# A hybrid decoder step on one core: reordered work at the first input tiles and at the last output tiles

## What is computed

```python
h = rms_norm(x, norm_mix_pre)
rq, rk, rv, rg, aq, ak, av, gr, ga = split_columns(h @ w_in, IN_WIDTHS)
# branch A: multi-scale retention; branch B: dilated window attention in three groups
mix = sigmoid(gr) * (r @ w_branch_ret) + sigmoid(ga) * (att_o @ w_branch_attn)
x = x + rms_norm(mix @ w_out, norm_mix_post)
u = rms_norm(x, norm_ffn_pre) @ w_ffn_up
c = conv_b + sum(conv_w[i] * ext[:, i:i + T] for i in range(3))
f = (gelu(c[..., :D_FF]) * c[..., D_FF:]) @ w_ffn_down
x = x + rms_norm(f, norm_ffn_post)       # y_prompt and y_sample
```

## Time and profile before

| what | value |
|---|---|
| median of 3 runs | 1087.83 us (1085.61 to 1088.73) |
| profiled execution, its own time | 1086.23 us |
| span of that execution, first to last instruction | 1084.4 us |
| mean granted TensorE clock | 0.981 of full speed |
| PE busy | 1014.0 us, 94% of the span |
| DVE, ACT, POOL busy | 541.8, 383.5, 197.3 us |

### The profile page before, as it was taken

How to read it: one execution, slowest core, us unless ns; L and a number is a source line. 1 busy time by engine, 2 the same in 40 slices (tenths; PEclk the granted TensorE clock), 3 DMA queues, 4 the chain that set the end, 5 groups by cost and what they waited for, 6 DMA issues and landing times.

```text
span 1084.4 us, 20154 instructions
## 1 busy us (share of the span) xinstructions
PE 1014.0 (94%) x7666; PEld 882.5 (81%) x7666; DVE 541.8 (50%) x865; ACT 383.5 (35%) x842; POOL 197.3 (18%) x382
## 2 busy tenths in 40 slices
PE   5999999999997799999998888999999999999994
PEld 3777777768875699998887668999999999777773
DVE  5353233423237777765116266676667666422214
ACT  5333231441431433323223364444444443212312
POOL 2102003414133234334310100000000000011003
PEclk9999999999998899999999989999999999999998
DMA  6744425426496566564651612545554544221322
GB/s 225 263 158 161 165 102 202 175 89 232 183 297 205 167 202 200 183 203 146 228 174 59 219 59 95 208 165 174 167 202 171 174 154 145 81 84 64 112 90 85
DMA packets 40768, 175.34 MB, mean 162 GB/s; under 512 B 7242, under 2 KB 7690, under 8 KB 39168
## 3 DMA queue, kind: packets, MB, share of 16 engines
q1 hardware_dynamic: 25472, 125.78, 33.4%
q0 software_dynamic: 15232, 48.65, 14.0%
HBM read 164.40 MB, written 54.05 MB: 201 GB/s over the span
## 4 chain that ended last, share of the span: by engine, by line
PE 78%; DMA 6%; ACT 6%; DVE 5%; issue 2%; POOL 2%; SPq 0%; DVEq 0%; ACTq 0%; POOLq 0%
PE bank L1280 10%; PE bank L1282 9%; PE bank L1281 9%; PE bank L1759 8%; PE bank L1760 8%; PE bank L1761 8%; PE bank L1353 4%; PE bank L1355 4%; PE bank L1354 4%; DMA qbc<-sample_queries 3%; PE bank L1299 3%; DMA wraw<-in_weights 2%; ACT whi L782 1%; DMA kvv<-in_cache_kv_g 1%; DVE wlo L1836 1%
## 5 line engine op out<-in xcount | busy, mean ns | idle before, releaser
L1836 DVE TENSOR_TENSOR wlo<-wraw,whi 128x1024 fp32r<-128x1024 f32 x89 | 108.9, 1225 | 353.2 <-ACT whi L782 353.1
L782 ACT ACTIVATE whi<-wraw 128x1024 fp32r<-128x1024 f32 x91 | 96.4, 1059 | 391.8 <-PE bank L1282 247.6
L1759 PE MATMUL bank<-T1h,whi 128*128 128x288 f32 (+1 forms) x704 | 202.4, 288 | 3.1 <-DVE T1l L1846 1.7
L1760 PE MATMUL bank<-T1l,whi 128*128 128x288 f32 (+1 forms) x704 | 203.6, 289 | 0.0
L1761 PE MATMUL bank<-T1h,wlo 128*128 128x288 f32 (+1 forms) x704 | 203.2, 289 | 0.0
L1280 PE MATMUL bank<-whi,T1h 128*128 128x512 f32 (+1 forms) x352 | 142.3, 404 | 7.7 <-DVE etmp L1981 7.6
L1281 PE MATMUL bank<-wlo,T1h 128*128 128x512 f32 (+1 forms) x352 | 137.1, 390 | 0.0
L1282 PE MATMUL bank<-whi,T1l 128*128 128x512 f32 (+1 forms) x352 | 136.7, 388 | 0.0
L1759 PEld LDWEIGHTS bank<-T1h,whi 128*128 128x128 f32 x704 | 133.0, 189 | 3.8 <-issue 1.9
L1760 PEld LDWEIGHTS bank<-T1l,whi 128*128 128x128 f32 x704 | 132.7, 189 | 0.0
L1761 PEld LDWEIGHTS bank<-T1h,wlo 128*128 128x128 f32 x704 | 132.3, 188 | 0.0
(11 more groups left out here) (302 smaller groups left out, 1828.0 us busy)
## 6 DMA issues: line engine op xcount, KB each, us to landing
wraw<-in_weights SPq DMA_DIRECT2D x142, 512.0 KB, 3.6
out_s_kv_g<-in_cache_kv_g SPq DMA_DIRECT2D x64, 511.0 KB
qbc<-sample_queries POOLq DMA_DIRECT2D x48, 256.0 KB, 4.7
kvk<-in_cache_kv_g POOLq DMA_DIRECT2D x32, 256.0 KB, 4.3
kvv<-in_cache_kv_g POOLq DMA_DIRECT2D x16, 512.0 KB, 6.0
out_s_kv_g<-in_cache_kv_g SPq DMA_DIRECT2D x16, 508.0 KB
S<-in_state_ret POOLq DMA_DIRECT2D x16, 256.0 KB, 6.8
out_s_ret<-S POOLq DMA_DIRECT2D x16, 256.0 KB, 4.0
```

Of the source, the lines that this page charges most:

```text
L782: nc.scalar.activation(w_halves(s)[0], wraw[:, s % 2, :], ACT.Copy).then_inc(w_hi, 1)
L1759: mm(dst, Wh, T1h[:, k, c], start=k == 0, stop=False)
L1760: mm(dst, Wh, T1l[:, k, c], start=False, stop=False)
L1836: v.tensor_tensor(lo, wraw[:, s % 2, :], hi.bitcast(F), ALU.subtract).then_inc(w_lo, 1)
```

## The change

At the start, ACT and DVE split tile i - 1 in round i, in place of tile i - 2; ACT copies weight slot 0 to `whi` in round 1 behind the root of tile 1 and ahead of the split of tile 0, and slot 1 in round 2 behind the split of tile 1. The loops are one round shorter. At the end, five things change. PE works on the last slot but one for tiles 0 and 1 before it waits for `wlo` of the last slot. The sample tile comes first in the norm's order (`LAST_ORDER`). The first half of the columns is multiplied by `gfin` during the last slots, and the second half before the root is there, so that after the root one instruction per half multiplies by the inverse root and adds the residual. POOL's additions are gone. The last tile's two halves are stored by two transfers.

```diff
+LAST_ORDER = (4, 0, 1, 2, 3)
...
@@ SP, the end
-        for i in range(TILES):
-            sp.wait_ge(y_ready, i + 1)
-            sp.wait_ge(y_half, i + 1)
+        for p, i in enumerate(LAST_ORDER):
             dst = ...
-            sp.dma_start(dst, fo[0:rows(i), i, :]).then_inc(y_out, 16)
-        sp.wait_ge(y_out, 16 * TILES)
+            parts = ((0, 512), (512, 1024)) if p == TILES - 1 else ((0, 1024),)
+            for c0, c1 in parts:
+                sp.wait_ge(y_ready, 2 * p + c1 // 512)
+                sp.dma_start(dst[:, c0:c1], fo[0:rows(i), i, c0:c1]).then_inc(y_out, 16)
+        sp.wait_ge(y_out, 16 * (TILES + 1))
@@ POOL, the end
-        for i in range(TILES):
-            pool.wait_ge(y_scaled, i + 1)
-            r = rows(i)
-            nc.gpsimd.tensor_tensor(fo[0:r, i, 0:512], fo[0:r, i, 0:512], xo[0:r, i, 0:512], ALU.add
-                                    ).then_inc(y_half, 1)
@@ ACT, roots(): the same work in LAST_ORDER
-            for i in range(TILES):
+            for p, i in enumerate(LAST_ORDER):
...
-                act.wait_ge(squared, i + 1)
+                act.wait_ge(squared, p + 1)
@@ ACT, the start
-        for i in range(TILES + 2):
+        for i in range(TILES + 1):
...
-            if i >= 2:
+            if i == 1:
+                w_split(0)
+            if i:
                 for half in range(2):
-                    split_evac(("x", i - 2, half), T1h, T1s, 4 * half, i - 2)
-            if i in (1, 2):
-                w_split(i - 1)
+                    split_evac(("x", i - 1, half), T1h, T1s, 4 * half, i - 1)
+            if i == 2:
+                w_split(1)
@@ PE, b_block()
-                pe.wait_ge(w_lo, slot + 1)
+                last_two = tail == 2 and s == n - 1
+                if not last_two:
+                    pe.wait_ge(w_lo, slot + 1)
...
+                if last_two:
+                    for i in range(2):
+                        for k in K[:per]:
+                            ones.append(part(i, *k)[0])
+                    pe.wait_ge(w_lo, slot + 1)
                 if s == n - 1 or late:
                     for i in tiles:
-                        for k in K:
+                        for k in K[per:] if last_two and i < 2 else K:
@@ DVE, the start
-        for i in range(TILES + 2):
+        for i in range(TILES + 1):
...
-            if i >= 2:
+            if i:
                 for half in range(2):
-                    split_evac(("x", i - 2, half), T1h, T1l, 4 * half, i - 2)
+                    split_evac(("x", i - 1, half), T1h, T1l, 4 * half, i - 1)
@@ DVE, the end (in the loop over s, the 22 slots of the last projection)
             if s < 11:
                 conv_rows(s)
-        dve.wait_ge(gfin_in, 16)
-        for i in range(TILES):
+            if 0 <= s - (2 * n - 1 - TILES) < TILES:
+                i = s - (2 * n - 1 - TILES)
+                dve.wait_ge(half_sq, 2 * TILES)
+                dve.wait_ge(gfin_in, 16)
+                step(v.tensor_tensor(fo[0:rows(i), i, 0:512], fo[0:rows(i), i, 0:512], gfin[0:rows(i), 0:512], ALU.mult))
+        for p, i in enumerate(LAST_ORDER):
             r = rows(i)
-            dve.wait_ge(y_rt, i + 1)
-            scaled(fo[:, i, :], fo, i, 10, gfin, y_scaled)
-            dve.wait_ge(y_scaled, i + 1)
-            v.tensor_tensor(fo[0:r, i, 512:1024], fo[0:r, i, 512:1024], xo[0:r, i, 512:1024], ALU.add
-                            ).then_inc(y_ready, 1)
+            rs = rs_n[0:r, 10 + i:11 + i]
+            dve.wait_ge(y_sq, p + 1)
+            src = P[i][:, :] if i < 4 else fo[0:r, 4, 512:1024]
+            step(v.tensor_tensor(fo[0:r, i, 512:1024], src, gfin[0:r, 512:1024], ALU.mult))
+            dve.wait_ge(y_rt, p + 1)
+            step(v.reciprocal(rs, rt_n[0:r, 10 + i:11 + i]))
+            for half in range(2):
+                c = slice(512 * half, 512 * half + 512)
+                v.scalar_tensor_tensor(fo[0:r, i, c], fo[0:r, i, c], rs, xo[0:r, i, c], ALU.mult, ALU.add).then_inc(y_ready, 1)
```

More of the change, by code:

```diff
@@ L451, in build_layer @@
     y_sq, y_rt, y_ready = sem("y_sq"), sem("y_rt"), sem("y_ready")
-    y_scaled, y_half = sem("y_scaled"), sem("y_half")
     y_out = sem("y_out")
```

## The result

The changed kernel took 1075.57 us, median of 4 runs (1074.61 to 1077.29), against 1086.72 (1084.05 to 1088.73) for the kernel before, now 4 runs with one at 1084.05 more than the 3 that the prediction knew: a ratio of 0.9888, 95% interval 0.9871 to 0.9906. The profiled execution's own time went from 1086.23 to 1076.47, its span from 1084.4 to 1074.7, 9.7 us less.

What follows compares the result with a forecast made beforehand. PE, busy 94% of the span, was taken to bound the kernel. Gains of 2.3 us at the start and 4.9 at the end, 7.2 together, from the median 1087.83 gave 1080.5 us, range 1077.5 to 1084.

Steps and rivals of the forecast that it cites:

- From there to the end of the span at 1084.4 it is 3.2 us, which I keep: Program's end: from the last store's landing at 1081.2 to the span's end, 3.2 us would stay unchanged.
- the forecast of the end's gain, 4.9: Program's end: without the start's gain, the span would end at 1079.5 in place of 1084.4, 4.9 us sooner.
- 1.3 of PE's 1.9 us buy nothing: Last 48 matmuls: PE starts them 1.9 us sooner, but DVE becomes the end's bound, so 1.3 us gain nothing.
- 4.3 to 5.2: Bounds of the end's gain in us, from landing 1.9 to 2.6 and DVE's 2.28 to 2.41 a tile.
- rival A: At the end DVE isn't the bound; PE and ACT are: end gains 6.1 us, all together 8.4; chance 0.12.
- 2.3 between 2.0 and 2.5: Start: the second slot's matmuls would begin 2.3 us sooner, chosen between two cases of when PE's rate rises.
- The case that I gave 2.0 for: Start: PE's matmul rate rises at the same moment as before, 18.3; the second slot gains 2.0 us.
- the case of 2.5: Start: PE's rate rises as long after its first matmul as before; second slot at 25.5, 2.5 us gained.
- Rival B: Middle: the start's 2.3 us are lost to a transfer or POOL's chain keeping its time; 4.9 left; chance 0.15.

Runs made afterwards that it cites:

- experiment 1: The kernel before with only the changed ACT and DVE loops at the start: 1085.57 us, ratio 0.9976.
- experiment 3: The changed kernel plus one 128x512 POOL addition released late, by the last tile's first half: 22.3 us from the start of the last sample matmuls to the span's end.
- experiment 4: The changed kernel plus one 128x512 POOL addition released early, by the sample tile's square: 19.2 us from the start of the last sample matmuls to the span's end.
- experiment 5: The changed kernel plus a 128x8 POOL memset released by the last tile's first half: 21.1 us from the start of the last sample matmuls to the span's end.
- experiment 6: The kernel before with POOL's five additions given to DVE, behind its own: 1084.92 us, ratio 0.9964.
- Experiment 7: The changed kernel with the five first-half multiplications by `gfin` two slots sooner: 1077.29 us, ratio 0.9893.
- experiment 11: The changed kernel with the first-half `gfin` multiplications moved into each tile's own sequence: 20.9 us from the start of the last sample matmuls to the span's end.
- experiment 2: The changed kernel with the start loops of the kernel before: 1079.65 us, ratio 0.9929.

## Why the prediction was wrong

**The step that failed** is the one of which it says "From there to the end of the span at 1084.4 it is 3.2 us, which I keep". These 3.2 us were no fixed part of the program's end. 2.8 of them were POOL's: the end of the span came 5.2 us after POOL's last addition in the kernel before, in experiment 1 and in experiment 3, and with POOL's additions gone only 0.4 us are left behind the landing (SP waits 0.2 where it waited 3.0). Experiments 3 to 6 show it from both sides: put a computation of 0.1 us back at a late time and the span ends 5.4 us behind it, take the additions out of the kernel before and the wait is gone. That is 2.8 us of the 3.2 by which the forecast of the end's gain, 4.9, fell short of the 8.1. Why POOL's end takes 5 us no run shows. The chain of the kernel before ended in POOL's addition, and the list of SP's waits had the 3.0 us with another queue as the releaser. I had read the first as no more than the way to the store; the second the prediction didn't look at.

**The end otherwise** was right. From the last sample matmuls to DVE's last instruction I had 1074.0 - 1057.63 = 16.4 us and it took 16.2; DVE is the bound (2.24 us a tile, 2.3 forecast), two multiplications stand behind the last split, and the landing is near 2.1 us. "1.3 of PE's 1.9 us buy nothing" was a little too much: without the fill it is 1.0 us longer, so half of PE's 2.0 buys nothing. The bounds "4.3 to 5.2" take the slow landing or the slow tile alone; both together, 2.6 and 2.41, give 3.9. Experiment 7 makes rival A's condition true: with DVE's queue 1.4 us shorter PE takes over at tile 3, and the end gains 1.1 more, about what the rival had (6.1 for 4.9). The Trainium skill's formula ("DMA: Bandwidth & Descriptors", "Anatomy of one DMA", fixed 2.0 us plus the bytes at 436 GB/s) would have had the 256 KB store at an estimated 2.6 us. The changed kernel's stores from SP's queue took 2.1, and 2.7 for 512 KB. The slope between the two, 0.6 us, agrees with it, the fixed part doesn't; the page has its figure from GpSimd's path.

**The start** was right in mechanism and order: first matmul behind POOL's `wlo` (13.6 forecast, 13.61 in experiment 1), then DVE's norm of tile 3 at its old place. I took 2.3 between 2.0 and 2.5; it is 2.4 with transfers landing as before, and 3.0 in the changed kernel's profiled execution, by the luck of its transfers. In the 11 profiled executions with the new start it went from 1.2 to 3.0, median 2.5. The 1.2 is experiment 11's, where tile 1 and slot 1 landed late: ACT took them up at 9.14 and 15.71, and at 8.34 and 14.37 in experiment 1. The case that I gave 2.0 for, PE's rate rising as late as before, is nearer to what experiment 1 had: its matmuls were 0.43 us apart up to 15.91 and 0.23 from 17.89 on, and the eight transposes between took 1.8 us where the next eight took 1.0. It gave 2.4 all the same, as DVE's work on tiles 2 to 4 came when I had it for the case of 2.5 and hid PE's delay. Rival B, a loss in the middle, did come in the changed kernel's profiled execution, 1.7 us, but not by its mechanism: no transfer kept its time, the clock did it.

**The sum.** 2.4 and 8.1 are 10.5 us, inside what the ratio's interval gives (10.2 to 14.0 of 1086.7) and nearer its lower end. In the profiled pair it is 3.0 - 1.3 + 8.1, but for rounding the 9.7 of the spans: from the second slot to the last sample matmuls it took 1.3 us longer, 1.7 lost at 217 us and 0.4 regained. With 0.4 in place of the 3.2 the prediction's own working gives 2.3 + 7.7 = 10.0 us. The medians are 11.2 apart; no experiment splits the last us, which is less than the middle varies by.

**Left open.** The half clock near 217 us came in 5 of the 11 runs that have the new start and in none of the 3 that have the old one; that is too few to say that the new start brings it. The half clock in the last 48 matmuls came in 2 of the 5 runs in which PE waits for the last `wlo` and in none of the 9 with the fill; it cost 1.5 us each time (28.35 against 26.8, 21.2 against 19.7). If that is no chance, the fill is worth more than its 1.0. The middle alone, from slot 2's copy to the last one, took from 1024.6 to 1029.8 us in these 14 runs, so a single execution can't show a change of 1 us there.

## What to carry to other kernels

Look at the end of the program for who arrives last at the place where all queues meet, not only for the last transfer: an engine's last instruction may end ahead of the last landing, by 2.0 us in the kernel before (1079.2 and 1081.2), and still set the end. Here that was POOL (whether by its late computation or by its late wait is open), and giving its small additions to DVE paid 2.8 us beyond the chain of additions itself. Where several queues work off the same few tiles, add up the busiest one (five times 2.24 us) before counting another's head start as a gain; and where single executions differ by some us, compare fixed stretches inside the traces. E repeats within 0.1 us where the clock holds (18.7 in the changed kernel and in experiment 2); the stretch up to the second slot does not, as it hangs on when transfers land.

## What the runs showed of the hardware

In the four runs in which POOL had a computation behind a late wait, the span ended 5.2 to 5.4 us after it, for an addition of 1.75 or 1.47 us as for a memset of 0.10 (the kernel before, experiments 1, 3 and 5). In the other ten runs, experiment 4 with an addition that ended 12.7 us before the end among them, SP waited 0.2 us for the other queues. Two DVE instructions that read two buffers of SBUF took 1.89 us beside an addition on POOL and 1.40 without it (experiment 4 and the changed kernel). In the middle of the program the granted clock fell to half for 3.4 to 10.2 us at a time, at five to seven places; in the traces of the kernels before and after, PE had waited in the 6 us ahead of each (it was busy for 1.2 to 4.6 of them). Which of the places, and how long, changed from run to run of kernels that are the same there, and the middle's length with it, by up to 5 us.
